# One state matrix instead of two, exclusive sums by subtraction, and 64-wide matmul halves in an RWKV-7 recurrence

## The reference

```
def rwkv7_scan(r, w, k, v, kk, a, s0):
    def step(s, inp):
        r_t, w_t, k_t, v_t, kk_t, a_t = inp
        sa = jnp.einsum('bhvk,bhk->bhv', s, -kk_t)
        s = s * w_t[:, :, None, :] + sa[..., None] * (kk_t * a_t)[:, :, None, :] + v_t[..., None] * k_t[:, :, None, :]
        return s, jnp.einsum('bhvk,bhk->bhv', s, r_t)
    xs = tuple(jnp.swapaxes(t.astype(F32), 0, 1) for t in (r, w, k, v, kk, a))
    s_fin, ys = lax.scan(step, s0, xs)
    return jnp.swapaxes(ys, 0, 1), s_fin
```

## Time and profile before

| | |
|---|---|
| median of 3 runs | 4945.96 us (4945.6 to 4948.31) |
| profiled execution | 4957.9 us, span 4956.0 us |
| the recurrence stage | from about 3043 to 3773 us of the span |
| PE / PE weight loads busy | 86% / 72% of the span |
| DVE / ACT / POOL busy | 53% / 31% / 15% |
| mean granted TensorE clock | 0.912 of full speed |

### The profile page before, as it was taken

How to read it: one execution, slowest core, us unless ns; L and a number is a source line. 1 busy time by engine, 2 the same in 40 slices (tenths; PEclk the granted TensorE clock), 3 DMA queues, 4 the chain that set the end, 5 groups by cost and what they waited for, 6 DMA issues and landing times. The chain is left out here.

```text
span 4956.0 us, 70950 instructions
## 1 busy us (share of the span) xinstructions
PE 4270.7 (86%) x27114; PEld 3547.5 (72%) x27114; DVE 2633.8 (53%) x4845; ACT 1526.3 (31%) x3235; POOL 741.6 (15%) x796
## 2 busy tenths in 40 slices
PE   5999999866999999699967576999985799989978
PEld 3899888555788877599966133888874699965646
DVE  3557774655343358411107696777754425546745
ACT  3233221633222235211114242334433411133423
POOL 1111111221000000000004012111112114423321
PEclk8999999777999999799988588999986899999998
DMA  4544432531211144322121484434424335543334
GB/s 158 165 141 139 146 127 78 195 138 60 59 51 42 34 153 166 102 86 86 65 107 49 165 299 158 105 98 112 108 65 132 124 106 173 182 147 101 100 98 136
DMA packets 430680, 589.38 MB, mean 119 GB/s; under 512 B 166297, under 2 KB 317201, under 8 KB 428771
## 3 DMA queue, kind: packets, MB, share of 16 engines
q1 hardware_dynamic: 382425, 418.41, 27.6%
q0 software_dynamic: 46336, 164.57, 8.9%
q10 hardware_dynamic: 1616, 2.36, 0.1%
HBM read 429.67 MB, written 155.57 MB: 118 GB/s over the span
## 5 line engine op out<-in xcount | busy, mean ns | idle before, releaser
L320 PE MATMUL g_in_g_acc<-g_in_g_whi,g_in_hi 128*128 128x444 f32 (+4 forms) x960 | 357.0, 372 | 16.6 <-DVE g_in_g_wlo L310 9.9
L321 PE MATMUL g_in_g_acc<-g_in_g_wlo,g_in_hi 128*128 128x444 f32 (+4 forms) x960 | 346.3, 361 | 0.0
L322 PE MATMUL g_in_g_acc<-g_in_g_whi,g_in_lo 128*128 128x444 f32 (+4 forms) x960 | 345.7, 360 | 0.0
L196 PE MATMUL g_even_acc<-g_even_w_hi,h_hi 128*128 128x384 f32 (+1 forms) x960 | 317.3, 331 | 19.5 <-DVE g_even_w_lo L238 19.5
L198 PE MATMUL g_even_acc<-g_even_w_lo,h_hi 128*128 128x384 f32 (+1 forms) x960 | 317.1, 330 | 0.0
L199 PE MATMUL g_even_acc<-g_even_w_hi,h_lo 128*128 128x384 f32 (+1 forms) x960 | 317.1, 330 | 0.0
L320 PE MATMUL g_odd_g_acc<-g_odd_g_whi,h_hi 128*128 128x344 f32 (+3 forms) x816 | 263.9, 323 | 31.9 <-DVE g_odd_g_wlo L310 16.8
L321 PE MATMUL g_odd_g_acc<-g_odd_g_wlo,h_hi 128*128 128x344 f32 (+3 forms) x816 | 261.8, 321 | 0.0
L322 PE MATMUL g_odd_g_acc<-g_odd_g_whi,h_lo 128*128 128x344 f32 (+3 forms) x816 | 261.7, 321 | 0.0
L1597 DVE SCALAR_TENSOR_TENSOR up_cv<-up_acc,up_taps,up_cv 128x1023 f32<-128x1023 f32 x88 | 112.8, 1282 | 279.7 <-ACT up_cv L1573 272.5
L214 DVE COPY g_even_o_buf<-g_even_acc 128x384 f32<-128x384 f32 (+1 forms) x60 | 32.1, 535 | 399.2 <-PE g_even_acc L199 399.2
(11 more groups left out here) (582 smaller groups left out, 10357.3 us busy)
## 6 DMA issues: line engine op xcount, KB each, us to landing
...
```

The costliest lines, as they stand in the source:

```text
L196: mm = pe.matmul(o, hi[:, k, tt], w_hi[:, par, k, :wd], start=k == 0, stop=not split and k == kc - 1)
L320: pe.matmul(bank[:, :wd], hi[:, k, tt], w_hi[:, st % 2, k, :wd], start=k == 0, stop=False)
L321: pe.matmul(bank[:, :wd], hi[:, k, tt], w_lo[:, st % 2, k, :wd], start=False, stop=False)
L322: op = pe.matmul(bank[:, :wd], lo[:, k, tt], w_hi[:, st % 2, k, :wd], start=False, stop=k == KC - 1)
```

## The change

- One state instead of two: `M` is now written by `m_out` as `Mc` plus the update, in the weighting of the middle of the tile, and `scale` makes the next `Mc` out of `M` by one factor per channel, the new `gain`: the decay of the second half of the previous tile of that direction times that of the first half of this one. `gain` (a product of 128 x 4 on GpSimd) and its wait are new; four of the eight instructions of `scale` go.
- With it the update needs the keys in the same weighting as `A` does, so `late_keys`, the tile `lat`, the third sum matmul and its exponential go. The weighted keys are kept for four units in `kb`, written by `weigh`.
- The exclusive sum is no longer a matmul: a new step `before` (VectorE) subtracts the log decays from the inclusive sum in PSUM, and `sums_out` waits for it.
- `right`, `u`, `out` and `m` are written as 64-wide halves of the stationary operand, one writing PSUM partitions 0 to 63 and the next 64 to 127. `m` computes only the blocks that are read.

```diff
-        sums[d, :, 0] = upto.astype(np.float32) - mid
-        sums[d, :, 1] = before.astype(np.float32) - mid
-        sums[d, :, 2] = 1.0 - upto
-        ends[d, :, 0], ends[d, :, 1] = 1.0, mid[:, 0]
+        sums[d] = upto.astype(np.float32) - mid
+        ends[d, :, 0], ends[d, :, 1] = 1.0 - mid[:, 0], mid[:, 0]
...
-              ("T0_out", 0), ("out", -1), ("pairs1_out", 2), ("solve3", 1), ("pairs3", 2), ("pairs2_out", 2), ("y_scale", 1), ("late_keys", 2), ("X1", 0),
-              ("m", -1), ("sums", 3), ("flip", 1), ("pairs3_out", 2), ("load_v", 2), ("scale", 0), ("X1_out", 0), ("out_out", -1), ("sums_out", 3),
-              ("m_out", -1), ("y_end", 1), ("y_load_z", 0), ("y_center", 0), ("y_square", 0), ("y_bonus", 0), ("T1", 0), ("late", 3), ("late_out", 3), ("T1_out", 0),
+              ("T0_out", 0), ("out", -1), ("pairs1_out", 2), ("solve3", 1), ("pairs3", 2), ("pairs2_out", 2), ("y_scale", 1), ("X1", 0),
+              ("m", -1), ("sums", 3), ("flip", 1), ("pairs3_out", 2), ("before", 3), ("load_v", 2), ("scale", 0), ("X1_out", 0), ("out_out", -1), ("sums_out", 3),
+              ("m_out", -1), ("y_end", 1), ("y_load_z", 0), ("y_center", 0), ("y_square", 0), ("y_bonus", 0), ("T1", 0), ("late", 3), ("late_out", 3), ("gain", 3), ("T1_out", 0),
...
-                if what == "late_keys":
-
-                    pool.wait_ge((s.in_f, s.in_b)[d], (i + 1) * (3 * DMA))
+                if what == "gain" and n >= 2:
                     pool.wait_ge(s.exps, 2 * n + 2)
 
-                    wait(pool, s.m_mm, n - 3)
-                    pool.tensor_tensor(lat[:, n % 4, 0], xd[:, d, 2], ex[:, 3], ALU.mult)
-                    pool.tensor_tensor(lat[:, n % 4, 1], xd[:, d, 1], ex[:, 3], ALU.mult)
+                    wait(pool, s.mc, n - 3)
+                    pool.tensor_tensor(gain[:, n % 4], ecol[:, (n - 2) % 4, :, 0], ecol[:, n % 4, :, 1], ALU.mult)
...
-                    pe.matmul(f[0][:], sums[:, d, 0, :], xd[:, d, 0, :], start=True, stop=True).then_inc(s.gsum, 1)
-                    pe.matmul(f[1][:], sums[:, d, 1, :], xd[:, d, 0, :], start=True, stop=True).then_inc(s.gsum, 1)
+                    pe.matmul(f[0][:], sums[:, d, :], xd[:, d, 0, :], start=True, stop=True).then_inc(s.gsum, 1)
                 if what == "late":
                     wait(pe, s.a_out, n * HN)
-                    pe.matmul(f[2][:], sums[:, d, 2, :], xd[:, d, 0, :], start=True, stop=True)
...
                     for b in range(4):
-                        pe.matmul(ru[:, b * P:(b + 1) * P], arT[:, a, b, 0, :], Mc[:, d, b, :], start=True, stop=False)
+                        for to in halves:
+                            pe.matmul(ru[to, b * P:(b + 1) * P], arT[:, a, b, 0, to], Mc[:, d, b, :], start=True, stop=False)
                         for h in (2 * b, 2 * b + 1):
-                            op = pe.matmul(ru[:, h * HD:(h + 1) * HD], A[:, a, h, 2, :], v[:, a, h * HD:(h + 1) * HD], start=False, stop=h % 2 == 1)
+                            for to in halves:
+                                op = pe.matmul(ru[to, h * HD:(h + 1) * HD], A[:, a, h, 2, to], v[:, a, h * HD:(h + 1) * HD], start=False, stop=h % 2 == 1)
...
                     for h in range(HN):
-                        op = pe.matmul(ru[:, h * HD:(h + 1) * HD], TF[:, d, h, :], R[:, h * HD:(h + 1) * HD], start=True, stop=True)
+                        for to in halves:
+                            op = pe.matmul(ru[to, h * HD:(h + 1) * HD], TF[:, d, h, to], R[:, h * HD:(h + 1) * HD], start=True, stop=True)
...
                     for b in range(4):
-                        pe.matmul(om[:, b * P:(b + 1) * P], lat[:, a, 0, b * P:(b + 1) * P], U[:, b * P:(b + 1) * P], start=True, stop=False)
-                        op = pe.matmul(om[:, b * P:(b + 1) * P], lat[:, a, 1, b * P:(b + 1) * P], v[:, a, b * P:(b + 1) * P], start=False, stop=True)
+                        for q, values in enumerate((U, v[:, a])):
+                            for to, h in enumerate((2 * b, 2 * b + 1)):
+                                hs = slice(h * HD, (h + 1) * HD)
+                                op = pe.matmul(om[halves[to], hs], kb[:, a, q, hs], values[:, hs], start=q == 0, stop=q == 1)
...
                 if what == "sums_out":
 
-                    wait(act, s.ew, n)
-                    act.wait_ge(s.gsum, 3 * n + 1)
+                    act.wait_ge(s.before, n + 1)
+                    act.activation(ex[:, 2], ex[:, 2], ACT.Exp)
                     act.activation(ex[:, 0], f[0][:], ACT.Exp)
                     act.activation(ex[:, 1], f[0][:], ACT.Exp, scale=-1.0)
-                    act.wait_ge(s.gsum, 3 * n + 2)
-                    act.activation(ex[:, 2], f[1][:], ACT.Exp)
...
+                    if n >= 2:
+                        act.wait_ge(s.gain, n - 1)
+                        act.wait_ge(s.o_mm, n - 1)
+                        act.wait_ge(s.m_out, n - 1)
+                        for b in range(4):
+                            act.activation(Mc[:, d, b, :], M[:, d, b, :], ACT.Copy, scale=gain[:, n % 4, b:b + 1])
+                        act.drain()
...
+                if what == "before":
+                    dve.wait_ge(s.gsum, 2 * n + 1)
+                    dve.tensor_tensor(ex[:, 2], f[0][:], xd[:, d, 0], ALU.subtract).then_inc(s.before, 1)
...
-                        dve.tensor_tensor(M[e, d, :, e], M[e, d, :, e], by_block(om)[e, :, e], ALU.add)
+                        dve.tensor_tensor(M[e, d, :, e], Mc[e, d, :, e], by_block(om)[e, :, e], ALU.add)
```

More of the change, by code:

```diff
@@ L2634, in rwkv_tables @@
     j, t = np.arange(P)[:, None], np.arange(P)[None, :]
-    sums = np.zeros((2, P, 3, P), np.float32)
+    sums = np.zeros((2, P, P), np.float32)
     ends = np.zeros((2, P, 2), np.float32)
@@ L2727, in half @@
         return image.rearrange("(h g x) -> g h x", g=2, x=HALF_IMAGE)[g, :, 0:HD * HD].rearrange("h (p t) -> p h t", p=HD)
-    with stage(nc, "rwkv", "const", "init", "in_f", "in_b", "v_f", "v_b", "gsum", "exps", "late", "ew", "turned0", "turned1", "turned_out", "cleared", "amat", "a_out", "mc",
+    with stage(nc, "rwkv", "const", "init", "in_f", "in_b", "v_f", "v_b", "gsum", "before", "exps", "gain", "ew", "turned0", "turned1", "turned_out", "cleared", "amat", "a_out", "mc",
                "zeroed", "a_st_f", "a_st_b", "dg_f", "dg_b", "solved", "flipped", "t_st_f", "t_st_b", "t_in_f", "t_in_b",
@@ L2736, in rwkv_stage @@
         xd = sb("xd", [P, 2, 3, 512])
-        sums = sb("sums", [P, 2, 3, P])
+        sums = sb("sums", [P, 2, P])
         ends = sb("ends", [P, 2, 2])
@@ L2741, in rwkv_stage @@
         eye = sb("eye", [NB * HN, BASE, BASE])
-        ex = sb("ex", [P, 4, 512])
+        ex = sb("ex", [P, 3, 512])
         ecol = sb("ecol", [P, 4, 4, 2])
-        ew = sb("ew", [P, 4, 512])
-        lat = sb("lat", [P, 4, 2, 512])
+        gain = sb("gain", [P, 4, 4])
+        ew = sb("ew", [P, 2, 512])
+        kb = sb("kb", [P, 4, 2, 512])
         arT = sb("arT", [P, 4, 4, 2, P])
@@ L2787, in _ @@
         def _(sp):
-            sp.dma_start(sums[:], t_sums.rearrange("d p n t -> p d n t")).then_inc(s.const, DMA)
+            sp.dma_start(sums[:], t_sums.rearrange("d p t -> p d t")).then_inc(s.const, DMA)
             sp.dma_start(ends[:], t_ends.rearrange("d p n -> p d n")).then_inc(s.const, DMA)
@@ L2796, in part @@
                     tile = tokens(i, d)
-                    wait(sp, s.gsum, (n - 1) * 3)
+                    wait(sp, s.gsum, (n - 1) * 2)
                     wait(sp, s.ew, n)
-                    wait(sp, s.late, n - 1)
                     done = (s.in_f, s.in_b)[d]
@@ L2935, in part @@
                         for b in range(4):
-                            op = pe.transpose(f[q][:, b * P:(b + 1) * P], ew[:, q, b * P:(b + 1) * P], ident[:])
+                            row = ew[:, q] if q < 2 else kb[:, a, q - 2]
+                            op = pe.transpose(f[q][:, b * P:(b + 1) * P], row[:, b * P:(b + 1) * P], ident[:])
                         op.then_inc(turned, 1)
@@ L3013, in part @@
                     for b in range(4):
-                        pe.matmul(ru[:, b * P:(b + 1) * P], arT[:, a, b, 1, :], Mc[:, d, b, :], start=True, stop=False)
+                        for to in halves:
+                            pe.matmul(ru[to, b * P:(b + 1) * P], arT[:, a, b, 1, to], Mc[:, d, b, :], start=True, stop=False)
                         for h in (2 * b, 2 * b + 1):
-                            pe.matmul(ru[:, h * HD:(h + 1) * HD], A[:, a, h, 1, :], U[:, h * HD:(h + 1) * HD], start=False, stop=False)
-                            op = pe.matmul(ru[:, h * HD:(h + 1) * HD], A[:, a, h, 3, :], v[:, a, h * HD:(h + 1) * HD], start=False, stop=h % 2 == 1)
+                            hs = slice(h * HD, (h + 1) * HD)
+                            for to in halves:
+                                pe.matmul(ru[to, hs], A[:, a, h, 1, to], U[:, hs], start=False, stop=False)
+                            for to in halves:
```

(17 more changed lines are left out.)

9 lines of the change are left out of this document (4 added, 5 removed).

## The result

The changed kernel takes **4885.31 us** (median of 4 runs, 4883.0 to 4887.68); the kernel before, beside it, 4945.78 us (4944.6 to 4948.31). The ratio is 0.987, with a 95% interval of 0.9857 to 0.9882: 60 us less. The profiled execution took 4883.0 us, with a span of 4881.3, a clock of 0.911, and PE busy 85%.

A forecast was written before the change was run, and what follows sets the result against it. PE's work was taken to bound the middle, waits between engines the end. Middle 61, normalisation -5, start 0, last units 12, clock -13: 55 us off 4957.9, so 4902.9; less 12 to the median, 4891 us, range 4866 to 4920.

The forecast's parts named there:

- What goes off PE: Per middle period, `sums`, `late`, `u`, `right`, `out` and `m` together lose 5.96 of 29.18 us of PE work.
- What comes in its place: Between `X1` and `right`, new PE gaps of 1.65 us before `T1` and 0.5 before `X2`; period falls 3.8 us.
- The five periods with normalisation work: Middle periods with DVE normalisation work ahead of `T1_out`, until now covered by PE: about 1 us each lost again, -5.
- The clock: In the middle, the new gaps lower PE's clock in about a third of the periods: 5 x 2.6 = 13 us lost.
- the end of the stage: Last four units, `right`, `u`, `out` and `m` on the chain, partly at half clock: 3 us each, 12 saved.
- The start: Start of the stage, DVE and DMA bound, the subtraction against the quicker `weigh`: 0 us.
- The median: Whole kernel: the profiled execution lies 12 us over the median of 4945.96, so 4902.9 becomes a forecast of 4891 us.
- 1: Rival: the new gaps in the middle leave PE's clock alone, 13 us more gained, 4878 us; chance 0.20.
- 2: Rival: PE's clock falls in nearly every middle period, 42 us lost instead of 13, 4920 us; chance 0.12.
- 3: Rival: long halves in `right` and `out` do not pair, or the DMA round trip shows; 4907 to 4918 us; chance 0.14.
- 4: Rival: halves in `right`, `u`, `out`, `m` do not run side by side; slower, about 5010 us; chance 0.04.
- What costs nothing: Off PE's path: DVE stays under PE, its products quicken without GpSimd's `late_keys`, and the triangles' DMA stays in time.

The follow-up runs named there:

- matmul_in_the_gap: The changed kernel with one more 512-column matmul, its result unread, at the start of `late`, in the gap ahead of `X2`: 4870.62 us, again 4872.33.
- sum_by_matmul: The changed kernel with the exclusive sum made by a second matmul right behind the first, and no subtraction: 4860.77 us.
- halves_only: The kernel before with only the 64-wide halves in `right`, `u`, `out` and `m`; two states, three sums and `late_keys` stay: 4890.84 us.
- whole_tiles: The changed kernel with `right`, `u`, `out` and `m` in 128-wide whole tiles again; the rest of the change stays: 5013.42 us.
- exclusive_after_t1: sum_by_matmul with the second matmul of the exclusive sum moved to the start of `late`, in the gap ahead of `X2`: 4853.64 us.
- g1_dma_order: exclusive_after_t1 with the store of the inverted blocks right behind `flip` and their load first: 4850.70 us.

## Why the prediction was right, and where not

Forecast 4891 us, range 4866 to 4920; measured 4885.3.

- **What goes off PE.** Right to 0.01 us in `right`, `u` and `m` (1.95, 1.08, 1.08 against 1.94, 1.07, 1.07). The long halves, for which no row had the form, cost 0.057 us against the 0.054 taken from streaming. `out` takes 2.89 us (3242.12 to 3245.01) against 2.96.
- **What comes in its place.** The gap ahead of `T1` is 1.47 us for 1.65, ended by L3183 as said; the second 0.42 for 0.5. The period was put at 25.4 us and is 25.36. The five periods with normalisation work were put at 5 us more; their gaps ahead of `X2` are 5.6 us longer in sum than five of 0.43.
- **The clock.** The forecast had 13 us for it, as five falls of 2.6, put down to "the new gaps". matmul_in_the_gap takes the falls away up to 3380; its middle is 13.4 us shorter in one pair of executions and 6.8 in the other, after it has itself cost 0.36 us in each of sixteen periods (6 us): so some 13 to 19 us hung on them, an estimate. In the plain periods a fall costs 1.55 us, not 2.6, and three or four of ten have one; the rest lies in the last six periods. So the 13 us were about right as a total and put together wrongly. And it is the stretch of the second, shorter gap that the falls need, not the long one: sum_by_matmul has them without the long gap, matmul_in_the_gap has the long gap without them. The rows that the prediction drew on had only gaps of 1.42 us and more, and could not tell this.
- **The sum** was 55 us between the profiled executions; they lie 74.9 apart. The middle was put at 61 - 5 - 13 = 43 and gave 47.0. **The step that was mis-sized is the end of the stage**: "3 us each (2 to 5): 12" for the last four units, beside 24.7 measured. halves_only alone gives 20.4 of it, and whole_tiles 1.2. The working behind it was right (`right`, `u`, `out` and `m` on the unit's own chain), but 0.88 + 0.86 + 1.64 + 0.82 = 4.2 us per unit at full clock, and more at a clock of 0.69 in that stretch before and 0.74 now, is 17 or more, and I took 12.
- **The start** was put at 0 and gave 1.8.
- **The median.** The forecast took 12 us off because the profiled execution of before lay 12 over its median; the one of after lies 2 under its own. That takes 14 of the 20 us that the traces differ by from the forecast back, and leaves the forecast 5.7 us too high. Part of the agreement at the median is thus luck of two single executions.
- **Rivals.** 1 and 2 (no falls, falls in nearly every period) mark what was measured from both sides. 3 hardly happened here (one wait of 0.45 us for the DMA, at 3184.23), but waited next door: once the first gap was gone, the DMA round trip showed. 4, the loss of about 5010 us, did not come: 0.029 us per narrow record. The Trainium skill's rule (TensorE: Matmul & The Clock Gate, Part 3, that a weight load overlaps a running matmul only when the row groups differ) is contradicted by these halves, which share their row groups: loads and matmuls are both busy 1.00 of 1.00 us while `u` runs.
- **What costs nothing.** GpSimd's products were said to slow DVE's without a price on PE. The slowdown is shown; its price is not nothing, 9.5 us at the median when it comes back. The Trainium skill (SBUF — State Buffer, on who interferes with whom) says that a VectorE instruction with two SBUF inputs contends with a GpSimd instruction that reads SBUF; the trace agrees, 1.53 us for 0.69.

What I had not seen is that the part of the change that drops sums and states brings nothing at the median: the changed kernel and halves_only are within their intervals. It frees 1.76 us of PE per period and opens 1.89 us of gaps. Beside the halves it does shorten a plain period at full clock, from 26.44 to 25.36 us, and PE no longer waits for VectorE's weighing there; but halves_only has no falls of the clock in its plain periods, and the falls take most of it back (the middle is 4.4 us shorter). Kept as a matmul, and put where PE would idle, the exclusive sum makes the kernel 32 us faster than the change (exclusive_after_t1, 4853.64); this and g1_dma_order are the fastest of all that were run.
